# Splitting the low halves of the weights between VectorE and GpSimd in a two-block transformer kernel

## The reference, cut to what matters

```python
xn = rms_norm(h, norm_in_g)
proj = jnp.einsum('btd,de->bte', xn, w_in)        # 1024 x 6144
...                                               # retention, LRU
h = h + jnp.einsum('bte,ed->btd', mixed, w_out)   # 2048 x 1024
# twice, for l in range(2):
... = jnp.split(h @ w_in[l], IN_SPLITS_2, axis=-1)
o = merge_branches(y_ml, y_ga, y_na, zg, w_branch[l], w_out[l])
f = conv_ffn(modulate(...), w_up[l], conv_w[l], conv_b[l], w_down[l])
```

## Time and profile before

| | |
|---|---|
| median of 3 runs | 1784.59 us (1779.61 to 1784.72) |
| the profiled execution's own time | 1784.72 us |
| its span, first to last instruction | 1782.9 us |
| mean granted TensorE clock | 0.989 |
| PE busy | 1716.7 us, 96% of the span |
| DVE busy | 1259.3 us, 71% |
| ACT busy | 844.4 us, 47% |
| POOL busy | 0.2 us |

### The profile page before, as it was taken

The page is one execution under the profiler, slowest core; times in us unless marked ns, Lnnn a source line. Parts: engine busy times, 40 slices in busy tenths (PEclk is TensorE's granted clock), DMA queues, the critical chain, the costliest instruction groups (busy, mean ns, idle before and its releaser), DMA issues.

```text
span 1782.9 us, 25794 instructions
## 1 busy us (share of the span) xinstructions
PE 1716.7 (96%) x10136; PEld 1470.9 (82%) x10136; DVE 1259.3 (71%) x2198; ACT 844.4 (47%) x1336; POOL 0.2 (0%) x4
## 2 busy tenths in 40 slices
PE   7989979999999999999999999999999999999998
PEld 7888878776788777888888888889778889989987
DVE  7889756774679698856877775247746686667874
ACT  6665444454333444344444442345463445546653
POOL 0000000000000000000000000000000000000000
PEclk9999999999999999999999999999999999999999
DMA  8546533142124344532435555224222344525553
GB/s 328 216 154 234 167 106 113 54 141 73 48 95 157 110 148 166 202 119 83 153 129 189 190 196 193 85 73 140 81 82 72 117 144 132 189 96 189 184 185 116
DMA packets 71976, 251.77 MB, mean 141 GB/s; under 512 B 7984, under 2 KB 12336, under 8 KB 71216
## 3 DMA queue, kind: packets, MB, share of 16 engines
q1 hardware_dynamic: 66384, 241.74, 40.1%
q10 hardware_dynamic: 5472, 8.39, 1.4%
HBM read 249.05 MB, written 1.05 MB: 140 GB/s over the span
## 4 chain that ended last, share of the span: by engine, by line
PE 77%; DVE 14%; ACT 5%; issue 3%; DMA 1%; ACTq 0%; DVEq 0%
PE bank L646 62%; PE bank L776 4%; DVE w_lo L1639 4%; PE bank L955 2%; PE bank L941 2%; PE bank L1028 2%; PE bank L932 1%; ACT w_hi L1115 1%; PE bank L739 1%; PE bank L1017 1%; DVE mod_w L1694 1%; DVE att L2174 1%; DMA w_raw<-in_weights 1%; DVE probT L1694 1%; DVE resid_x L2053 1%
## 5 line engine op out<-in xcount | busy, mean ns | idle before, releaser
L1639 DVE TENSOR_TENSOR w_lo<-w_raw,w_hi 128x1024 fp32r<-128x1024 f32 x356 | 428.3, 1221 | 271.1 <-ACT w_hi L1115 269.8
L1115 ACT ACTIVATE w_hi<-w_raw 128x1024 fp32r<-128x1024 f32 x356 | 368.4, 1054 | 330.5 <-PE bank L646 284.5
L646 PE MATMUL bank<-hT_hi,w_hi 128*128 128x512 f32 (+1 forms) x1280 | 448.1, 350 | 5.0 <-DVE w_lo L1639 2.6
L646 PE MATMUL bank<-hT_hi,w_lo 128*128 128x512 f32 (+1 forms) x1280 | 439.2, 343 | 0.0
L646 PE MATMUL bank<-hT_lo,w_hi 128*128 128x512 f32 (+1 forms) x1280 | 438.9, 343 | 0.0
L646 PEld LDWEIGHTS bank<-hT_hi,w_hi 128*128 128x128 f32 x1280 | 244.1, 191 | 34.5 <-issue 4.3
L646 PEld LDWEIGHTS bank<-hT_hi,w_lo 128*128 128x128 f32 x1280 | 243.9, 191 | 28.2
L646 PEld LDWEIGHTS bank<-hT_lo,w_hi 128*128 128x128 f32 x1280 | 244.1, 191 | 27.7 <-issue 1.3
L1694 DVE SCALAR_TENSOR_TENSOR mod_w<-mod_w,c_rows 128x1024 f32<-128x1024 f32 x96 | 116.9, 1218 | 2.7 <-DMA mod_w<-in_mod_weights 2.7
L646 PE MATMUL bank<-w_hi,hT_hi 128*128 128x512 f32 x272 | 115.2, 423 | 1.6 <-DVE gkT_lo L2214 1.4
L646 PE MATMUL bank<-w_lo,hT_hi 128*128 128x512 f32 x272 | 107.2, 394 | 0.0
(11 more groups left out here) (369 smaller groups left out, 2931.5 us busy)
## 6 DMA issues: line engine op xcount, KB each, us to landing
w_raw<-in_weights SPq DMA_DIRECT2D x356, 512.0 KB, 3.8
mod_w<-in_mod_weights SPq DMA_DIRECT2D x96, 512.0 KB, 3.8
nbias<-in_window_bias ACTq DMA_DIRECT2D x32, 128.0 KB, 2.7
resid_c<-in_ctx ACTq DMA_DIRECT2D x2, 1024.0 KB, 5.0
c_rows<-in_conditions SPq DMA_DIRECT2D x1, 1024.0 KB, 5.6
gatew<-in_gate_weights SPq DMA_DIRECT2D x1, 1024.0 KB, 11.5
decay<-in_decay SPq DMA_DIRECT2D x1, 1024.0 KB, 5.8
out<-resid_x ACTq DMA_DIRECT2D x2, 512.0 KB, 2.6
```

The costliest lines, as they stand in the source:

```text
L646: mm = pe.matmul(held[key][:, oc], st, mv_, start=(opens and k == 0 and t == 0 and i == 0), stop=(closes and k == tiles - 1 and t == 2), s ...
L1115: a.activation(w_hi[:, p % RING].rearrange("p k n -> p (k n)"), w_raw[:, p % RING, :], ACT.Copy).then_inc(hi_ready, 1)
L1639: v.tensor_tensor(w_lo[:, p % RING].rearrange("p k n -> p (k n)"), w_raw[:, p % RING, :], w_hi[:, p % RING].rearrange("p k n -> p (k n)"). ...
```

## The change

`w_lo` is made by two engines. GpSimd gets a queue of its own that subtracts the first of the two row tiles of every piece (columns 0 to 511, semaphore `lo0_ready`), as soon as `w_hi` is there and the piece four before has been used. DVE keeps the second tile (semaphore `lo1_ready`) where its one instruction stood. Whoever waited for `lo_ready` (SP before a load, PE before a piece) now waits for both. Besides, ACT's calls of `split_hi` in the LRU part ask for one piece fewer after the `xc` exponentials, and for none between the `lru_r` ones.

```diff
                 if p >= RING:
-                    sp.wait_ge(lo_ready, p - RING + 1)
+                    sp.wait_ge(lo0_ready, p - RING + 1)
+                    sp.wait_ge(lo1_ready, p - RING + 1)
...
+        @block.gpsimd
+        def _(pool):
+            def split_lo(i, s, first):
+                pool.wait_ge(hi_ready, i * RING + s + 1)
+                if not first:
+                    pool.wait_ge(piece_used, (i - 1) * RING + s + 1)
+                nc.gpsimd.tensor_tensor(w_lo[:, s, 0, :], w_raw[:, s, 0:COLS], w_hi[:, s, 0, :].bitcast(F32),
+                                        ALU.subtract).then_inc(lo0_ready, 1)
+            for s in range(RING):
+                split_lo(0, s, True)
+            with pool.Fori(1, NPIECES // RING) as i:
+                for s in range(RING):
+                    split_lo(i, s, False)
...
                             pe.wait_ge(hi_ready, at + p + 1)
-                            pe.wait_ge(lo_ready, at + p + 1)
+                            pe.wait_ge(lo0_ready, at + p + 1)
+                            pe.wait_ge(lo1_ready, at + p + 1)
...
                 if n % 4 == 3:
-                    split_hi(21 + n // 4)
+                    split_hi(20 + n // 4)
             act.wait_ge(*A.last())
             for n in range(HEADS):
                 a.activation(lru_r[:, n, :], lru_r[:, n, :], ACT.Exp, ...)
-                if n % 4 == 3:
-                    split_hi(23 + n // 4)
             tok(4, v1, ACT.Copy)
...
                     dve.wait_ge(hi_ready, p + 1)
-                    v.tensor_tensor(w_lo[:, p % RING].rearrange("p k n -> p (k n)"), w_raw[:, p % RING, :],
-                                    w_hi[:, p % RING].rearrange("p k n -> p (k n)").bitcast(F32), ALU.subtract).then_inc(lo_ready, 1)
+                    v.tensor_tensor(w_lo[:, p % RING, 1, :], w_raw[:, p % RING, COLS:KP * COLS],
+                                    w_hi[:, p % RING, 1, :].bitcast(F32), ALU.subtract).then_inc(lo1_ready, 1)
```

More of the change, by code:

```diff
@@ L371, in build @@
     hi_ready = es.enter_context(nc.semaphore("hi_ready"))
-    lo_ready = es.enter_context(nc.semaphore("lo_ready"))
+    lo0_ready = es.enter_context(nc.semaphore("lo0_ready"))
+    lo1_ready = es.enter_context(nc.semaphore("lo1_ready"))
     piece_used = es.enter_context(nc.semaphore("piece_used"))
@@ L833, in out_last @@
                                 pe.wait_ge(hi_ready, n + 1)
-                                pe.wait_ge(lo_ready, n + 1)
+                                pe.wait_ge(lo0_ready, n + 1)
+                                pe.wait_ge(lo1_ready, n + 1)
                                 pe.wait_ge(*drained_at(("ry", 5 + KP * p)))
```

## The result

The changed kernel took 1809.69 us in the median (1807.59 to 1811.08), the kernel before 1784.65 us beside it: 1.0142 times as long, 95% interval 1.0115 to 1.0168. I had forecast 1775.8 us with a range up to 1796. (A ratio here is an estimate over all executions of both kernels; the quotient of the two medians differs from it by up to 0.0016.) The profiled execution of the changed kernel has a span of 1809.3 us, 26.4 more than that of the kernel before.

The account below looks back on a forecast made before the run. PE, 96% busy, bounds the large products of layer 1; DVE's w_lo holds 62 us of the chain. Terms 0.3 + 0 - 3.6 - 5.6 = -8.9 took 1784.7 to 1775.8 us, range 1764 to 1796.

Parts of the forecast that it names:

- What bounds the kernel: Whole kernel: PE is 96% busy with 66 us idle; a shorter w_lo pays mainly in the first 250 us.
- DVE's half: All 356 w_lo instructions: 692 ns in place of 1221, saving 0.53 us each, 188 us of DVE's busy time.
- POOL's half: All 356 pieces: 1.2 us per POOL operation, bounds 0.69 and 2.86 us; POOL about 430 us busy.
- Do the two hinder each other: SBUF reads of DVE and POOL: no hindrance or only one reads at a time, priced by DVE's two-input time share, 0.44.
- the 0 for 92 to 187 us: From 92 to 187 us: 15.4 us lost to exclusion equals 15.4 us saved, so 0 taken; ACT's delay absorbed.
- 34 to 47 us: PE's wait at 46.32 us: shorter w_lo save 2.1, two delayed mod_w products cost 2.4; +0.3 us taken, between -1.5 and +1.5.
- The ACT edit: Near 92 us: piece 23 rounded later, PE resumes at 94.7 instead of 92.23, 2.5 us late, absorbed by idle time.
- 187 to 250 us: Nine w_lo in the chain from 187 to 250 us: eight save 4.2 us, one ends 0.67 later; -3.6 us.
- behind it: Behind 250 us: 21 w_lo instructions in the chain worth at most 11.3 us, half taken; -5.6 us.
- a sign of being wrong: Behind 250 us: forecast is wrong if PE's idle time doesn't fall although w_lo has left the chain.
- No hindrance: Rival, whole kernel: both engines read freely, -21 us, 1764 us; chance 0.12.
- POOL goes first: Rival: DVE loses over 0.53 us per POOL operation on average, lengthening DVE's stage; 1797 us; chance 0.21.

Follow-up runs that it names:

- the run without reads: Changed kernel with POOL writing zeros instead of subtracting, at the same 356 places, queue written out flat; 1752.24 us, ratio 0.9853 of the kernel before.
- the run with half left out: Changed kernel with POOL zeroing its half of all four w_lo buffers once, then resting; 1751.62 us, ratio 0.9837 of the kernel before.
- experiment 3: Changed kernel where POOL zeroes its w_lo half once at the start and does nothing afterwards; 1751.62 us beside 1780.61 for the kernel before.

## Why the prediction was wrong, step by step

- **What bounds the kernel: right in kind.** DVE's chain costs PE time from 92 to 250 us and in places behind; 700 to 1150 us loses under 3 us to 26 us more on DVE.
- **DVE's half: right in its own length.** 690 ns where nothing disturbs it (forecast 692). The whole relief is 1259.3 - 1079.0 = 180 us of busy time (forecast 188).
- **POOL's half: right in its own length.** 1.27 to 1.28 us undisturbed (taken 1.2); with the waits for DVE it is 1.67 in the mean, and POOL is busy 591 us where I had said 430. The estimate from the Trainium skill (GPSIMD Engine Reference, "Performance versus the Vector engine") was 1.1; the measurement is 0.2 us above it.
- **Do the two hinder each other: the term that failed.** The exclusion itself was in the prediction, in the rule of the Trainium skill (SBUF — State Buffer, "Who interferes with whom"); the trace agrees with it in kind (1.81 us at 1581 us) and the run without reads too. What failed was my price for it, 1.2 x 0.44 = 0.53 us for each POOL operation, and with it the 0 for 92 to 187 us, where I had 15.4 us lost against 15.4 saved. Two things were wrong in it.

  First, the share of 0.44 counts four rows. The same view has eight more of operations with two inputs in SBUF:

```profile
L1810 DVE TENSOR_TENSOR xc<-xc,glT 128x256 f32<-128x256 f32 x8 | 2.9, 418 | 0.0
L1815 DVE TENSOR_TENSOR mix_lo<-xc,mix_hi 128x256 fp32r<-128x256 f32 x8 | 2.8, 414 | 0.0
...
L1787 DVE TENSOR_TENSOR onrm<-onrm,sg 128x256 f32<-128x256 f32 x6 | 2.5, 425 | 1.5 <-ACT sg L1195 1.2
L1859 DVE TENSOR_TENSOR lru_i<-lru_i,xc 128x2048 f32<-128x2048 f32 x1 | 2.3, 2279 | 0.0
...
L1722 DVE TENSOR_TENSOR qT<-qT,rot_tmp 128x512 f32<-128x512 f32 x2 | 1.4, 692 | 0.1
L1722 DVE TENSOR_TENSOR kT<-kT,rot_tmp 128x512 f32<-128x512 f32 x2 | 1.4, 692 | 0.1
L1719 DVE TENSOR_TENSOR qT<-qT,rot 128x512 f32<-128x512 f32 x2 | 1.4, 682 | 0.0
L1719 DVE TENSOR_TENSOR kT<-kT,rot 128x512 f32<-128x512 f32 x2 | 1.4, 677 | 0.0
```

  They add 16.1 us, so the share is 58 of 95 us, 0.61, and 29 x 1.2 x 0.61 = 21 us against 15.4 saved: the same sum, with all its rows, has this stage lose about 6 us.

  Second, a share of time is too low a price even so. The groups of the changed kernel from 92 to 200 us, which is nearly the same work:

```profile
L1658 DVE TENSOR_TENSOR w_lo<-w_raw,w_hi 128x512 fp32r<-128x512 f32 x28 | 30.1, 1098 | 5.1 <-ACT w_hi L1136 5.0
L1713 DVE SCALAR_TENSOR_TENSOR probT<-mod_w,c_rows 128x1024 f32<-128x1024 f32 x8 | 15.1, 1889 | 0.1
L1713 DVE SCALAR_TENSOR_TENSOR mod_w<-mod_w,c_rows 128x1024 f32<-128x1024 f32 x8 | 10.8, 1352 | 0.0
L1840 DVE TENSOR_TENSOR_SCAN xc<-lru_r,lru_i 128x256 f32<-128x256 f32 x8 | 8.1, 1046 | 0.0
```

  28 x (1098 - 690) + 8 x (1889 - 1216) + 8 x (1352 - 1220) + 8 x (1046 - 674) ns = 11.4 + 5.4 + 1.1 + 3.0 = 20.9 us lost against 28 x 0.53 = 14.8 saved. I also matched every DVE instruction with the same one in the run with half left out: `mix_lo`, `lru_i` and `kT` bring the loss in this stretch to 24.6 us, 0.88 us for each of the 28 POOL operations. It lies in 26 lengthened DVE instructions of 0.95 us each, not far from the 1.12 that one POOL operation can cost at most. So nearly every POOL operation met one, and met it early. 23 of the 28 had themselves waited for a DVE operation, and so got their turn just when DVE's next one began; a share of time leaves that out. I had argued that where DVE comes to a piece late, POOL has long finished. It does come late here (in 19 of the 28 pieces over 1.3 us after POOL began), but POOL's operation then meets what DVE does in the meantime; only 2.0 of the 24.6 us are DVE's half waiting for POOL's half of the same piece.

  From 700 to 1150 us it is the other way round. DVE follows ACT closely, one `hi_ready` releases both engines, and 46 of the 66 us lost there are DVE's half waiting for POOL's half of the same piece. Over the whole kernel 227 DVE instructions are lengthened by 208 us in all (as busy time 1280.3 - 1079.0 = 201 us), more than the 180 of relief: 69 us are halves of the same piece, 52 us `w_lo` against POOL's half of another piece, 87 us other operations.
- **34 to 47 us: mis-sized.** I took +0.3 (at most +1.5). Both `mod_w` products let a POOL operation pass (2.31 us each in place of 1.22), and PE, which had resumed at 46.32 us, resumes at 48.14, 1.8 us later.
- **The ACT edit: right by itself,** to 0.02 us (94.7 forecast, 94.68 measured), and its 2.5 us were taken up on the way. In the changed kernel PE resumes only at 97.87 us, 3.2 us later still, as PE was 2.5 us late already (its 520th matmul starts at 90.44 us, 87.91 before) and ACT's square root begins at 93.06, not at the 90.5 of my reckoning. From the timeline of PE in the changed kernel:

```profile
97.87 0.76 PE L665 MATMUL bank<-w_hi,xT_hi 128*128 128x512 f32 x1 [7.03 <-ACT w_hi L1136]
```

- **187 to 250 us: mis-sized; behind it: wrong sign.** Between its 1200th and 1400th matmul (208 to 256 us before) PE gains 1.3 us, not 3.6. Behind that it loses another 13 us where I had -5.6, and its idle time behind 250 us rises from 35 to 51 us, which I had named as a sign of being wrong. That term presupposed that POOL is either long done or harmless. But where DVE has waited for `w_hi` both start together, as at 1581 us, and the one that goes second, or what stands behind it, is late.
- **The ceiling: too low.** "No hindrance" was to give 1764; it gives 1752. Of the 34.5 us between the two profiled executions 20 are PE's idle time, about what I had counted; what I left out are the 14 us of its busy time, which go with the higher granted clock. How much of that clock is the edit's doing, and how much the spread between executions (experiment 3), stays open. Likewise in the changed kernel: 20.7 of its 26.4 us are idle time, 5.7 busy time.
- **The rivals.** "POOL goes first" was the true one: DVE loses 201 us / 356 = 0.56 us to each POOL operation, beyond the 0.53 that I gave as the point where the sign turns. I gave it 1797 us and 0.21. My argument against it (DVE waits 139 times and would be first) fails twice: POOL was first often enough that 68 of DVE's halves waited for POOL's half of the same piece, and it overlooks the operations behind the first one.

## What to carry to other kernels

Before work goes to a second engine, ask whether the two can read at the same time at all. If they can't, the shared work costs the sum of both parts, and POOL's part is the slower one: 0.69 + 1.12 us here against 1.22 for the undivided operation. And price a collision by following one operation through its whole length: from 92 to 200 us a POOL operation cost DVE 0.88 us, where the share of busy time gave 0.53 as I counted it and 0.73 with every row. Where one semaphore releases both engines, as in the feed-forward part, they meet at the start.

## What the runs showed of the hardware

- The time by which a POOL operation holds up a DVE product of two SBUF operands (1217 ns by itself) is a little less than its own length. At most 2337 - 1217 = 1.12 us for a subtraction of 512 columns (1.27 us undisturbed); 0.58 us for a subtraction of 256 (0.72 us); 0.42 us for a copy of 512 (0.61 us); nothing for a memset of 512 (0.53 us). The maximum for the subtraction stands in this row of the changed kernel's view of that line:

```profile
L1713 DVE SCALAR_TENSOR_TENSOR probT<-mod_w,c_rows x24: 1210/1219/2337, 22.9 to 935.4; 128x1024 f32<-128x1024 f32 x24
```

- DVE operations with an operand in PSUM went on beside POOL unchanged: 171 of them ran while a POOL operation was under way, and none took over 8 ns more than the longest of its form in the kernel before (34 of them are convolution taps, L2532, at most 484 ns in both kernels). None of the 227 lengthened instructions reads PSUM.
- PE's busy time for the same 10136 matmuls goes with the granted clock of the execution: 1702.5 us at 0.995 (half left out), 1716.7 at 0.989 (before), 1722.5 at 0.986 (changed). That less idle time is what raises the clock isn't shown: the kernel before by itself ran at 0.987 to 0.996.
